# Tanh gates, packed meta-key transposes, paired index heads and a single triangle in a hybrid attention and mixture-of-experts layer

## What is computed

```python
proj = rms_norm(h) @ w_in           # qa ka va fa cq ckv kr kidx iw ga gb
log_f_cum = cumsum(log_sigmoid(fa + b_forget))
o_a = fox_attention(qa, ka, va, log_f_cum)          # 8 heads, causal
q_idx = rope_partial(rms_norm(cq) @ w_qidx)         # 4 index heads of 64
dots = einsum('bqhd,bkd->bhqk', q_idx, k_idx)
iscore = einsum('bqh,bhqk->bqk', idx_w, relu(dots))
top_idx = top_k(iscore, 64)                         # keys that branch b may see
o_b = dsa_attention(..., top_idx)                   # 8 heads, latent keys
merged = sigmoid(ga) * (o_a @ w_branch_a) + sigmoid(gb) * (o_b @ w_branch_b)
h = h + merged @ w_out
h = h + moe_ffn(rms_norm(h))        # top 4 of 32 experts, 12.6 MB of weights each
out = rms_norm(h)[meta tokens dropped]
```

## Time and profile before

| what | value |
|---|---|
| median of 3 runs | 1164.3 us (1163.63 to 1164.34) |
| profiled execution, its own time | 1166.17 us |
| profiled execution, span from first to last instruction | 1164.3 us |
| busy share of the span: PE, PEld, DVE, ACT, POOL | 95%, 45%, 29%, 17%, 1% |
| moved by DMA | 433.74 MB, 373 GB/s over the span |
| mean granted TensorE clock | 0.985 of full |

### The profile page before, as it was taken

How to read it: one execution, slowest core, us unless ns; L and a number is a source line. 1 busy time by engine, 2 the same in 40 slices (tenths; PEclk the granted TensorE clock), 3 DMA queues, 4 the chain that set the end, 5 groups by cost and what they waited for, 6 DMA issues and landing times. The chain is left out here.

```text
span 1164.3 us, 13587 instructions
## 1 busy us (share of the span) xinstructions
PE 1107.9 (95%) x5490; PEld 528.7 (45%) x5490; DVE 332.2 (29%) x774; ACT 203.7 (17%) x359; POOL 14.4 (1%) x27
## 2 busy tenths in 40 slices
PE   9999999999999989898999999999898989899987
PEld 6878888554343434343434343434343434343433
DVE  2256443131323131313132223132222222222223
ACT  2437781031101010101010100010000000001002
POOL 3010000000000000000000000000000000000000
PEclk9999999999999999999999998999999999999999
DMA  9914237859999999999999999999999999999994
GB/s 304 284 35 131 87 110 306 344 208 423 422 433 431 430 432 431 432 432 432 429 432 431 432 431 431 432 431 431 432 432 432 432 430 432 431 426 429 427 428 183
DMA packets 40475, 433.74 MB, mean 373 GB/s; under 512 B 3240, under 2 KB 19778, under 8 KB 23284
## 3 DMA queue, kind: packets, MB, share of 16 engines
q1 hardware_dynamic: 38880, 429.45, 88.2%
q0 software_dynamic: 960, 2.30, 0.6%
q10 hardware_dynamic: 596, 1.45, 0.4%
HBM read 432.13 MB, written 1.05 MB: 372 GB/s over the span
## 5 line engine op out<-in xcount | busy, mean ns | idle before, releaser
L1757 PE MATMUL psum<-arena 128*64 128x512 f32 x1016 | 231.8, 611 | 10.2 <-DMA arena<-in_w_gate_up 10.2
L1757 PE MATMUL psum<-ring,arena 128*64 128x512 f32 x968 | 218.8, 607 | 7.0 <-DMA ring<-in_w_gate_up 7.0
L1757 PEld LDWEIGHTS psum<-arena 128*64 128x64 f32 x1016 | 72.5, 140 | 162.0 <-issue 145.8
L1757 PEld LDWEIGHTS psum<-ring,arena 128*64 128x64 f32 x968 | 68.5, 139 | 149.9 <-issue 139.7
L1773 PE MATMUL psum<-ring,arena 128*64 128x512 f32 x544 | 122.6, 602 | 11.6 <-DMA ring<-in_w_down 8.6
L1208 DVE TENSOR_TENSOR arena<-psum,biasT 128x512 f32<-128x512 f32 x64 | 44.3, 692 | 298.3 <-PE psum L1722 294.0
L871 DVE TENSOR_TENSOR arena<-psum,vT 128x512 f32<-128x512 f32 (+1 forms) x42 | 28.4, 681 | 337.0 <-PE psum L1649 326.3
L1773 PE MATMUL psum<-arena 128*64 128x512 f32 x480 | 106.5, 595 | 9.7 <-DMA arena<-in_w_down 9.7
L785 ACT ACTIVATE arena<-psum 128x1024 f32<-128x1024 f32 x32 | 32.7, 1023 | 333.0 <-PE psum L1757 316.9
L1232 DVE TENSOR_TENSOR h<-h,psum 128x1024 f32<-128x1024 f32 x64 | 75.3, 1218 | 16.0 <-PE psum L1798 14.0
L1773 PEld LDWEIGHTS psum<-ring,arena 128*64 128x64 f32 x544 | 42.3, 138 | 80.6 <-issue 77.4
(11 more groups left out here) (233 smaller groups left out, 762.2 us busy)
## 6 DMA issues: line engine op xcount, KB each, us to landing
arena<-in_w_gate_up SPq DMA_DIRECT2D x27, 4096.0 KB, 29.3
ring<-in_w_gate_up SPq DMA_DIRECT2D x24, 4096.0 KB, 30.0
arena<-in_w_down SPq DMA_DIRECT2D x13, 4096.0 KB, 30.0
ring<-in_w_down SPq DMA_DIRECT2D x12, 4096.0 KB, 29.8
ring<-in_w_gate_up SPq DMA_DIRECT2D x8, 2048.0 KB, 26.8
ring<-in_w_in SPq DMA_DIRECT2D x14, 1024.0 KB, 12.4
arena<-in_w_gate_up SPq DMA_DIRECT2D x7, 2048.0 KB, 30.5
arena<-in_w_gate_up SPq DMA_DIRECT2D x13, 1024.0 KB, 15.1
```

The lines of the kernel that those rows point to most:

```text
L1757: ins = mm(bank[home + n][h * CAP:(h + 1) * CAP, :], xg[:, c, e * CAP:(e + 1) * CAP], w[:, h * D + n * 512:h * D + (n + 1) * 512], start=c ...
```

## The change

Five edits, all in the mixer stage:

- The gates are computed as tanh of half the argument in place of sigmoid. The merge then multiplies by (tanh + 1) with a scalar_tensor_tensor in place of a tensor_tensor, and the missing factor 0.5 is put into ScalarE's copies of the attention outputs.
- The probabilities of the 16 meta keys are normalised by a VectorE instruction of their own into a buffer `prm`, where four items lie side by side at 32 columns each. Every fourth item transposes them with one 128-column transpose; VectorE then makes the four small copies together, ahead of that item's large copy. The other keys are normalised by the existing instruction, now 16 columns narrower.
- `qiT` holds two index heads on 128 partitions: two transposes a tile in place of four, and a ScalarE copy of 256 columns in place of 512. The index keys are copied twice, to partitions 0 to 63 and 64 to 127. The `dots` matmuls of two heads stand next to one another on the two halves of the array's rows and write two banks; both banks are waited for ahead of the first.
- VectorE adds the identity to the strict triangle once (`tri`), and `FT` multiplies with that sum alone: three matmuls fewer.
- The layout of `late` and `pT` changes to suit; the sum of the sizes is the same.

```diff
-                copy_out(("qiT", t), qiT[0:ID, :, t * P:(t + 1) * P],
-                         job_bank(("qiT", t))[0:ID, :].rearrange("p (h k) -> p h k", h=IH))
+                copy_out(("qiT", t), qiT[:, :, t * P:(t + 1) * P],
+                         job_bank(("qiT", t))[:, 0:IH // 2 * P].rearrange("p (h k) -> p h k", h=IH // 2))
...
-                sc.activation(dst, bank[6 + n % 2].rearrange("p (c k) -> p c k", c=2), ACT.Copy).then_inc(s_on, 1)
+                sc.activation(dst, bank[6 + n % 2].rearrange("p (c k) -> p c k", c=2), ACT.Copy,
+                              scale=0.5).then_inc(s_on, 1)
...
-                    empty_end(sc.activation(dst, job_bank(name)[:, 0:SEQ], ACT.Sigmoid), name)
+                    empty_end(sc.activation(dst, job_bank(name)[:, 0:SEQ], ACT.Tanh, scale=0.5), name)
...
+            v.tensor_tensor(tri, ltri, ident, ALU.add).then_inc(s_tri, 1)
...
-            v.tensor_copy(kiT[0:ID, :], job_bank(("kkT", 0))[0:ID, 0:KEYS])
+            for n in range(2):
+                v.tensor_copy(kiT[n * ID:(n + 1) * ID, :], job_bank(("kkT", 0))[0:ID, 0:KEYS]).then_inc(s_kiT, 1)
...
-                    v.tensor_scalar(pr[:, k % 3, 0:w], pr[:, k % 3, 0:w], rk[:, 32 + k:33 + k], None,
+                    heads_meta = slice(k % 8 * 32, k % 8 * 32 + META)
+                    v.tensor_scalar(prm[:, heads_meta], pr[:, k % 3, 0:META], rk[:, 32 + k:33 + k], None, ALU.mult)
+                    v.tensor_scalar(pr[:, k % 3, META:w], pr[:, k % 3, META:w], rk[:, 32 + k:33 + k], None,
                                     ALU.mult).then_inc(s_pn, 1)
...
-                    v.tensor_copy(dst[0:META, 384 + t * P:384 + (t + 1) * P], src[0:META, 256:384])
+                    if k % 4 == 3:
+                        for m in range(4):
+                            v.tensor_copy(pT[2 * (pair % 2) + m // 2][0:META, 384 + m % 2 * P:384 + (m % 2 + 1) * P],
+                                          src[32 * m:32 * m + META, 256:384])
                     empty_end(v.tensor_copy(dst[:, t * P:t * P + (t + 1) * P], src[:, 0:(t + 1) * P]), ("PT", k))
...
-                empty_end(v.tensor_tensor(dst, dst, job_bank(name)[:], ALU.mult), name)
+                empty_end(v.scalar_tensor_tensor(dst, dst, 1.0, job_bank(name)[:], ALU.add, ALU.mult), name)
...
-                terms = [(lf[0:rows, t, :], ltri[0:rows, 0:rows]), (lf[0:rows, t, :], ident[0:rows, 0:rows])]
+                terms = [(lf[0:rows, t, :], tri[0:rows, 0:rows])]
...
-                for h in range(IH):
-                    ins = tr(job_bank(name)[0:ID, h * P:(h + 1) * P],
-                             qtok[:, t, 768 + h * ID:768 + (h + 1) * ID], ident)
+                for h in range(IH // 2):
+                    ins = tr(job_bank(name)[:, h * P:(h + 1) * P],
+                             qtok[:, t, 768 + 2 * h * ID:768 + 2 * (h + 1) * ID], ident)
...
-                for h in range(IH):
-                    name = ("dots", t, h)
-                    fill_begin(pe, name)
-                    fill_end(mm(job_bank(name)[:, 0:WIDTH[t]], qiT[0:ID, h, t * P:(t + 1) * P],
-                                kiT[0:ID, 0:WIDTH[t]], start=True, stop=True), name)
+                for h in range(0, IH, 2):
+                    for u in range(2):
+                        fill_begin(pe, ("dots", t, h + u))
+                    for u in range(2):
+                        name = ("dots", t, h + u)
+                        part = slice(u * ID, (u + 1) * ID)
+                        fill_end(mm(job_bank(name)[:, 0:WIDTH[t]], qiT[part, h // 2, t * P:(t + 1) * P],
+                                    kiT[part, 0:WIDTH[t]], start=True, stop=True), name)
...
-                fill_end(tr(job_bank(name)[0:META, 256:384], pr[:, i % 3, 0:META], ident), name)
+                if i % 4 == 3:
+                    ins = tr(job_bank(name)[:, 256:384], prm[:, i // 4 % 2 * P:(i // 4 % 2 + 1) * P], ident)
+                fill_end(ins, name)
```

More of the change, by code:

```diff
@@ L192, in build @@
         late = take(IH * SEQ + 512)
-        qiT = late[:, 0:IH * SEQ].rearrange("p (h k) -> p h k", h=IH)
+        qiT = late[:, 0:IH * SEQ // 2].rearrange("p (h k) -> p h k", h=IH // 2)
         wuv = late[:, IH * SEQ:IH * SEQ + 512]
@@ L214, in build @@
         kaT = take(HEADS * KEYS).rearrange("p (h k) -> p h k", h=HEADS)
-        pT = take(4 * 384)
+        pT = take(2 * 640)
+        prm = take(2 * P)
         pr = take(3 * KEYS)
@@ L239, in build @@
         pT = [half[:, n * 640:(n + 1) * 640] for half in (pT, late) for n in range(2)]
+        tri = pT[0][:, 0:P]
         logf = logf.rearrange("p (a n) -> p a n", a=4)
@@ L322, in build @@
         s_nf = sem("forget_row_beside_keys")
+        s_tri = sem("inclusive_triangle_ready")
+        s_kiT = sem("index_keys_in_both_halves")
         s_kk = sem("index_and_rope_keys_ready")
@@ L1063, in _ @@
                 b_ = gbS[:, 2 * m:2 * m + 2, :].rearrange("p c k -> p (c k)")
-                ins = v.tensor_tensor(b_, b_, job_bank(name)[:], ALU.mult)
+                ins = v.scalar_tensor_tensor(b_, b_, 1.0, job_bank(name)[:], ALU.add, ALU.mult)
                 empty_end(ins, name)
@@ L1437, in _ @@
             pe.wait_ge(s_logf, 1)
+            pe.wait_ge(s_tri, 1)
             lf = logf[:, 2, :].rearrange("p (t h) -> p t h", t=3)
@@ L1483, in _ @@
                 fill_begin(pe, name)
-                for h in range(IH):
-                    ins = tr(job_bank(name)[0:ID, h * P:(h + 1) * P],
-                             qtok[:, t, 768 + h * ID:768 + (h + 1) * ID], ident)
+                for h in range(IH // 2):
+                    ins = tr(job_bank(name)[:, h * P:(h + 1) * P],
+                             qtok[:, t, 768 + 2 * h * ID:768 + 2 * (h + 1) * ID], ident)
                 fill_end(ins, name)
+            pe.wait_ge(s_kiT, 2)
             wait_emptied(pe, ("kkT", 0))
@@ L1541, in transposed @@
                 for k in range(t + 1):
-                    tr(job_bank(name)[:, k * P:(k + 1) * P], pr[:, i % 3, META + k * P:META + (k + 1) * P],
-                       ident)
-                fill_end(tr(job_bank(name)[0:META, 256:384], pr[:, i % 3, 0:META], ident), name)
+                    ins = tr(job_bank(name)[:, k * P:(k + 1) * P],
+                             pr[:, i % 3, META + k * P:META + (k + 1) * P], ident)
+                if i % 4 == 3:
+                    ins = tr(job_bank(name)[:, 256:384], prm[:, i // 4 % 2 * P:(i // 4 % 2 + 1) * P], ident)
+                fill_end(ins, name)
             def values(j):
```

## The result

Over 20 runs each, the changed kernel takes 1166.74 us (1164.91 to 1167.5) and the one before 1164.83 us (1163.45 to 1166.8). The ratio is 1.0015, 95% interval 1.0009 to 1.0021: 1.8 us slower by the ratio and 1.9 by the medians, where 1.7 us faster was forecast. It lies outside the forecast range of 1160.3 to 1164.4.

The account below looks back on a forecast made before the run. The expert weight stream was taken as the bound, its start set by the mixer stage, where TensorE binds the loop. Loop start 0.6 plus loop 1.1 made 1.7 us off the 1164.3 median: 1162.6 us, range 1160.3 to 1164.4.

Parts of the forecast that it names:

- What bounds the kernel: Expert stage runs at its weight stream's rate; the change gains only what it brings the first refill at 252.41 forward.
- Tanh gates, nothing: Attention loop: removing 31 table loads, 39.8 us of ScalarE time, gains nothing because TensorE binds.
- Triangle, 0.5 us: `FT`, ahead of the loop: three matmuls fewer save 0.5 us (0.3 to 0.7) on TensorE, and it counts.
- Index heads, 0.2: `dots`, ahead of the loop: of 2 us leaving TensorE only 0.2 (0 to 0.5) counts, through an earlier first relu.
- TensorE's idle at the first transpose: First transpose of probabilities: TensorE would be there 1.3 us or more before VectorE, the heads' remaining saving becoming idle time.
- Start of the loop: Attention loop starts earlier by 0.5 + 0.2 - 0.1 = 0.6 us (0.2 to 1.1).
- Meta transposes: Attention loop: 2.6 us of transposes out, 1.3 and 0.2 lost again, so 1.1 us gained (-0.4 to 2.6).
- The stall: TensorE's wait at `values` for VectorE's bunched copies: 0.18 us in seven of eight cases, 1.3 us; bounds 0 to 0.4 each.
- A gap at `values` over 0.4 us: Sign that the prediction is wrong; gaps near 0.2 us ahead of `values` in the loop would show it right.
- The rival on the slower side: Attention loop: bunched copies become the bound, 0.45 us per small copy, stall 1.16 us, 1169.4 us in all; chance 0.05.
- The last item's turns, 0.2 lost: Loop's end, items 30 and 31: TensorE follows VectorE, so the last two saved transposes buy nothing, 0.2 us lost.
- The clock: Router's half-rate clock, about 1.6 us: falling behind the refill gives 1161.0 (chance 0.2), falling in the loop 1164.2 (0.1).

Follow-up runs that it names:

- e4: The kernel before with only the tanh gates and their merge edits: 1164.2 us, ratio 0.9998 to the kernel before.
- e7: The kernel before with only the packed meta keys, sigmoid gates kept: 1167.81 us against 1164.45, ratio 1.0026.
- e2: The changed kernel with the meta keys normalised, transposed and copied item by item again: 1164.39 us, ratio 0.9994 to the kernel before.
- e5: The changed kernel with all four small copies reading PSUM partitions 0 to 15; run once, read by trace: value product 3.01 us after the scores' start.
- e6: The changed kernel with all four small copies reading PSUM partitions 32 to 47; run once, read by trace: value product 3.26 us after the scores' start.

## Why the prediction was wrong

- **What bounds the kernel**: right. The distance from the first refill to the end is 911.0 to 912.3 us in all 14 profiles, 911.9 before and 912.2 after, so the span of an execution follows its first refill to within 1.3 us.
- **Tanh gates, nothing**: right alone (e4), wrong in company (e7 against after, 0.8 us). I checked the cover against TensorE only, and not against the VectorE that the packing would load.
- **Triangle, 0.5 us**: right. `FT` to the next group went from 2.19 to 1.70 us, and with it (e2, no packing) the first transpose came 0.58 us sooner, of which 0.04 is the index heads'. No run undid it alone.
- **Index heads, 0.2**: the mechanism was right, the size 0.04. TensorE's idle at the first transpose was forecast as 1.3 us or more and is 1.59. Start of the loop: 0.6 forecast, 0.42 measured.
- **Meta transposes**: this is the step that failed. The 2.6 us were there. The stall was forecast as 0.18 us and is 0.57, because of one term: four steps at 0.20 are 0.80, and measured 1.18. Seven times the missing 0.39 us is the 2.7 us by which the loop missed its forecast, all but 0.1. Everything else of that sum holds: first copy at +1.66 forecast and +1.67 measured, the value product at +3.01 forecast and +3.01 in e5, the same release of 0.15 us. A gap at `values` over 0.4 us was the prediction's own sign of being wrong, and 0.49 to 0.50 of idle time stands there. The trace of before had no copy with another start partition, and I took the price of the nearest one and left the other end of the bound at 0.4 for the whole stall; its range should have held a copy that doesn't overlap its predecessor, 0.27 us and more, which the rows already showed.
- **The rival on the slower side** named this mechanism and its turning point, a stall of 0.43 us, and got 0.05. With the price of such a copy open, that was too little. Its size was wrong too: it priced a copy that reads partitions 32, 64 or 96 at 0.45 us, by the partition, where 0.295 was measured, and by the change. Its sum takes four dearer copies where three read such partitions; with three the stall is 0.91 us and the time 1167.7, not 1169.4.
- **The range** was a little too narrow by its own terms: the lower bounds of start and loop, 0.2 and -0.4, make 0.2 us lost, 1164.5, and it ended at 1164.4.
- **The last item's turns, 0.2 lost**: about right, 0.3 by the starts above; e5's loop is 85.63 us, against 86.83 - 2.6 + 7 x 0.16 + 0.2 = 85.55.
- **The clock**: right as a size (1.5 us between before and after from first load to refill), and the longer idle time at the first transpose, 1.59 us, brought no fall into the loop, whose clock is 1.00. Whether a profile has the fall is luck, and that before's had it and after's hadn't says nothing of the change. It was wrong as a basis: before's profile had both the fall and a late start, 1166.17 us of its own time where the median of 20 runs is 1164.83. Carrying a difference from it to the median was harmless for the change, but reading the new profile against it by their ends would have shown a gain.

## What to carry to other kernels

Bunching small copies ahead of a wait moves them from where they were hidden to where nothing hides them, so count the time left between the release and the need, with the dearest plausible step, before counting what is saved. On VectorE the small copies that read PSUM from changing start partitions didn't overlap here, 0.29 us a piece in place of 0.20; give such copies to an engine with time to spare, or order them by start partition. When a saving lands in front of a wait, look for work of the same engine that can be put ahead of the wait: one moved half product gave 1.5 us.

## What was not expected of the hardware

- A VectorE copy of 16x128 from PSUM steps by 0.20 us behind a copy with the same first partition and by 0.28 to 0.30 behind one with another (e5, e6, after).
- Two row halves at once: the 16 records of `dots` take 1.79 us in place of 2.98, a ratio of 0.60, near the scatter's 0.56 from which it was foreseen.
- The start differs from one execution to the next: `FT` begins at 56.42 to 57.84 us in the 14 profiles, and the landing of the first weights (0.20 and 0.76 us of waiting in the two rows above) is a part of it. It isn't the whole: e7, at 57.84, waits 0.49 us there.
